# A decoder step on one core: prompt's compression moved ahead of the key stage, stick-breaking sums in rounded parts

## The reference

```python
def sb_attend(q, k, v, q_pos, k_pos):
    z = einsum('bqhd,bshd->bhqs', q, k) / sqrt(HEAD_DIM)
    mask = k_pos[None, :] < q_pos[:, None]
    log_1m = where(mask, log_sigmoid(-z), 0.0)
    after = cumsum(log_1m, axis=3, reverse=True) - log_1m
    a = where(mask, exp(log_sigmoid(z) + after), 0.0)
    return einsum('bhqs,bshd->bqhd', a, v)

def nsa_compress(kv, w_ck1, w_ck2, w_cv1, w_cv2, pe_k, pe_v):
    # 16-token chunks, blocks of two chunks: 31 blocks for the prompt, 127 for a sample
    ...
    kc = mlp(blocks[:, :, :, 0], pe_k, w_ck1, w_ck2)   # silu((x + pe) @ w1) @ w2
    vc = mlp(blocks[:, :, :, 1], pe_v, w_cv1, w_cv2)
```

## Time and profile before

| | |
|---|---|
| runs | 1195.89, 1203.27, 1191.61 us; median 1195.89 |
| profiled execution | 1194.02 us, of which the span of the profile 1192.2 us |
| mean granted clock of TensorE | 0.942 |
| PE, DVE, ACT busy | 91%, 51%, 32% of the span |

### The profile page before, as it was taken

The page is one execution under the profiler, slowest core; times in us unless marked ns, Lnnn a source line. Parts: engine busy times, 40 slices in busy tenths (PEclk is TensorE's granted clock), DMA queues, the critical chain, the costliest instruction groups (busy, mean ns, idle before and its releaser), DMA issues.

```text
span 1192.2 us, 22997 instructions
## 1 busy us (share of the span) xinstructions
PE 1084.8 (91%) x8348; PEld 951.0 (80%) x8348; DVE 605.8 (51%) x1026; ACT 382.4 (32%) x707; POOL 70.7 (6%) x83
## 2 busy tenths in 40 slices
PE   3996998988999999999999888999999999999993
PEld 2896998877888888555556557999999999999993
DVE  4331674776787782565345446445543335553332
ACT  4111112332333333545444445322231112321223
POOL 2000001111111110000000000110000000000002
PEclk9999997999899895899989998999999999999997
DMA  6529217999999942166766661323332333332221
GB/s 245 181 79 221 78 40 201 260 254 258 277 259 276 249 154 82 56 202 195 227 201 204 208 222 37 89 71 88 88 106 89 90 87 88 90 101 72 89 72 72
DMA packets 180131, 177.61 MB, mean 149 GB/s; under 512 B 13063, under 2 KB 140676, under 8 KB 177700
## 3 DMA queue, kind: packets, MB, share of 16 engines
q1 hardware_dynamic: 178610, 171.33, 50.3%
q10 hardware_dynamic: 1458, 5.43, 1.4%
HBM read 170.83 MB, written 10.06 MB: 152 GB/s over the span
## 4 chain that ended last, share of the span: by engine, by line
PE 64%; SPq 19%; issue 7%; DMA 4%; ACT 3%; DVE 3%; POOL 0%; POOLq 0%; ACTq 0%; DVEq 0%
PE bank L658 60%; SPq L572 4%; PE bank L662 4%; SPq L493 4%; SPq L532 3%; SPq L535 3%; SPq L486 2%; SPq L560 2%; DMA low_arena<-in_cache_nsa_slc_kv_dram 1%; DMA high_arena<-in_w_in_dram 1%; DMA high_arena<-in_x_sample_dram 1%; ACT low_arena L1528 1%; DMA high_arena<-in_cache_sb_kv_dram 0%; SPq L499 0%; SPq L501 0%
## 5 line engine op out<-in xcount | busy, mean ns | idle before, releaser
L658 PE MATMUL bank<-high_arena 128*128 128x254 f32 (+9 forms) x1864 | 238.7, 343 | 15.7 <-DMA high_arena<-in_cache_sb_kv_dram 6.9
L658 PEld LDWEIGHTS bank<-high_arena 128*128 128x128 f32 (+5 forms) x1864 | 185.7, 152 | 53.2 <-issue 13.5
L662 PE MATMUL bank<-low_arena 128*128 128x128 f32 (+3 forms) x658 | 104.8, 302 | 35.5 <-DMA low_arena<-in_cache_nsa_slc_kv_dram 18.0
L2083 DVE TENSOR_TENSOR w_low<-high_arena,w_high 128x1024 fp32r<-128x1024 f32 x72 | 90.1, 1251 | 85.4 <-ACT w_high L1465 73.8
L662 PEld LDWEIGHTS bank<-low_arena 128*128 128x128 f32 (+3 forms) x658 | 84.9, 160 | 46.8 <-issue 29.6
L1465 ACT ACTIVATE w_high<-high_arena 128x1024 fp32r<-128x1024 f32 x72 | 76.3, 1060 | 114.8 <-PE bank L658 113.7
L658 PE MATMUL bank<-a_high,w_high 128*128 128x256 f32 (+1 forms) x512 | 104.2, 285 | 5.3 <-issue 2.9
L658 PE MATMUL bank<-h_high,w_high 128*128 128x256 f32 (+1 forms) x512 | 103.6, 284 | 1.8 <-DVE h_low L2110 1.8
L658 PE MATMUL bank<-h_high,w_low 128*128 128x256 f32 (+1 forms) x512 | 103.8, 284 | 0.0
L658 PE MATMUL bank<-h_low,w_high 128*128 128x256 f32 (+1 forms) x512 | 103.8, 284 | 0.0
L658 PE MATMUL bank<-a_low,w_high 128*128 128x256 f32 (+1 forms) x512 | 103.7, 284 | 0.0
(11 more groups left out here) (207 smaller groups left out, 1533.8 us busy)
## 6 DMA issues: line engine op xcount, KB each, us to landing
low_arena<-in_cache_sb_kv_dram SPq DMA_DIRECT2D x128, 256.0 KB, 4.6
high_arena<-in_cache_sb_kv_dram SPq DMA_DIRECT2D x128, 256.0 KB, 3.4
high_arena<-in_cache_nsa_cmp_kv_dram SPq DMA_DIRECT2D x128, 128.0 KB, 5.0
high_arena<-in_w_up_dram SPq DMA_DIRECT2D x32, 512.0 KB, 4.0
high_arena<-in_w_down_dram SPq DMA_DIRECT2D x32, 512.0 KB, 4.2
high_arena<-in_w_in_dram SPq DMA_DIRECT2D x10, 1136.0 KB, 5.5
low_arena<-in_cache_nsa_slc_kv_dram SPq DMA_DIRECT2D x128, 64.0 KB
high_arena<-in_cache_nsa_slc_kv_dram SPq DMA_DIRECT2D x128, 64.0 KB, 2.3
```

Source lines behind the costliest of these rows:

```text
L658: return T.matmul(out, lhsT=l, rhs=r, start=start, stop=stop, **k)
L662: return T.transpose(out, in_, ident[0:n, 0:n])
L2083: V.tensor_tensor(w_lo_r[u], w_raw[u], w_hi[u], ALU.subtract).then_inc(sem(f"w_lo{u}"), 1)
```

## The change

1. The prompt's compression becomes the first unit of the key stage on PE, ACT, DVE and POOL. It is called `compress(0, 1, ...)`, and the semaphore counts of the samples' units are shifted by what it adds (`past`). Its chunks are loaded to the second buffer (`nat[1][0]`), by SP, after the stores of the prompt's compressed, selected and window keys and ahead of the store of its stick-breaking keys and values. POOL's permutations of a sample's first half now wait for PE's transposes of the unit before.
2. `sb_sum` no longer multiplies f32 soft sums with f32 masks. `sb_soft` writes to one buffer `sums`; ACT rounds it to fp32r (`sb_high`, into `z_parts`), DVE subtracts the rounded part from it and leaves the rest in fp32r too (`sb_low`, into `sums_low`), and PE multiplies both parts with rounded copies of the masks (`ntri_r`, `nones_r`): twice as many products, of one pass each. The rounded and the rest each have one buffer for a pair, in place of two buffers of sums. The masks are rounded by ACT once the sample scores have arrived. `rankA` moves to another place in memory.

```diff
-        spb = [z[:, NT, 0:2560].rearrange("p (h c) -> p h c", h=2), view(late_at, 2, 1280)]
+        sums = view(r_at, 2, 512)
+        sums_hi_r = rounded("z_parts", z_at, T5, COLS)[:, NT, 0:2560].rearrange("p (h c) -> p h c", h=2)
+        sums_hi = sums_hi_r.bitcast(F32)
+        sums_lo_r = rounded("sums_low", late_at, 2, 1280)
...
# SP
+            sp.wait_ge(sem("cmp_stored"), 16)
+            sp.dma_start(nat[1][0][0:2 * (NCP + 1)].rearrange("p t k h d -> p (t k h d)"),
+                O["cmp_p"][0, 0].rearrange("(c t) k h d -> c (t k h d)", t=CH // 2)).then_inc(sem("nat_in10"), 16)
             sp.dma_start(O["sb_p"][0, 0].rearrange("(t p) k h d -> p t (k h d)", p=P), z[:, 0:NT, O_KS:O_KS + 1024]).then_inc(sem("sb_stored"), 16)
...
-                        sp.wait_ge(sem("perm"), i * 8 + (4 * u + half) + 1)
+                        sp.wait_ge(sem("perm"), i * 8 + (4 * u + half + 2) + 1)
...
             load_keys(3, 0, True)
-            sp.wait_ge(sem("cmp_stored"), 16)
-            sp.wait_ge(sem("perm"), 4 * 6 + 3 + 1)
-            sp.dma_start(nat[0][0][0:2 * (NCP + 1)].rearrange("p t k h d -> p (t k h d)"),
-                O["cmp_p"][0, 0].rearrange("(c t) k h d -> c (t k h d)", t=CH // 2)).then_inc(sem("nat_in00"), 16)
             load_keys(3, 1, False)
...
# PE
+            compress(0, 1, lambda: None)
             with pe.Fori(0, 4) as i:
                 for u in range(2):
...
                     compress(i * 2 + u, 2, lambda: todo.pop(0)())
-            compress(B, 1, lambda: None)
...
             def sb_sum(m):
                 pr, i, n = sb_unit(m)
-                pe.wait_ge(sem("sb_sp"), m + 1)
-                for h in range(2):
-                    out = bank[2 * (m % 2) + h]
-                    ins = mm(out[:, 0:n], ntri, sp_tile(pr, i)[:, h], False, i == 3, skip_group_check=True)
-                    for j in range(3, i, -1):
-                        ins = mm(out[:, (j - i) * P:n], nones, sp_tile(pr, j)[:, h], False, j == i + 1, skip_group_check=True)
+                if m == 0:
+                    pe.wait_ge(sem("masks_in"), 2)
+                for part, ready in ((sums_hi_r, "sb_hi"), (sums_lo_r, "sb_lo")):
+                    pe.wait_ge(sem(ready), m + 1)
+                    for h in range(2):
+                        out = bank[2 * (m % 2) + h]
+                        for j in range(i, NT):
+                            ins = mm(out[:, (j - i) * P:n], nones_r if j > i else ntri_r, sp_tile(part, j)[:, h], False,
+                                     part is sums_lo_r and j == NT - 1, skip_group_check=True)
                 ins.then_inc(sem("sb_c"), 1)
...
# ACT
+            act.wait_ge(*signal("c_sc", 1))
+            for dst, name in ((ntri_r, "ntri"), (nones_r, "nones")):
+                ins = S.activation(dst, K(name), ACT.Copy)
+            ins.then_inc(sem("masks_in"), 1)
...
+            def sb_high(m):
+                pr, i, n = sb_unit(m)
+                act.wait_ge(sem("sb_sp"), m + 1)
+                if m:
+                    act.wait_ge(sem("sb_c"), m)
+                S.activation(sp_tile(sums_hi_r, i), sums[:, :, 0:n], ACT.Copy).then_inc(sem("sb_hi"), 1)
...
                     sb_exp(s - 1)
+                if s < SB_U:
+                    sb_high(s)
...
# DVE
                 dve.wait_ge(sem("sb_ln"), m + 1)
-                if pr >= 2:
-                    dve.wait_ge(sem("sb_c"), 4 * (pr - 1))
-                V.scalar_tensor_tensor(out=sp_tile(pr, i), in0=bank_pair(2 * (m % 2))[:, :, 0:n], scalar=0.0,
+                if m:
+                    dve.wait_ge(sem("sb_lo"), m)
+                V.scalar_tensor_tensor(out=sums[:, :, 0:n], in0=bank_pair(2 * (m % 2))[:, :, 0:n], scalar=0.0,
                                        in1=ebuf[:, m % 2, :, 0:n], op0=ALU.max, op1=ALU.add).then_inc(sem("sb_sp"), 1)
+            def sb_low(m):
+                pr, i, n = sb_unit(m)
+                dve.wait_ge(sem("sb_hi"), m + 1)
+                V.tensor_tensor(sp_tile(sums_lo_r, i), sums[:, :, 0:n], sp_tile(sums_hi, i), ALU.subtract).then_inc(sem("sb_lo"), 1)
...
                     acc_out(VALUE_ENDS.index(s - 1))
+                if 1 <= s < SB_U + 1:
+                    sb_low(s - 1)
                 small_steps(s)
...
# POOL
+            pool.wait_ge(sem("nat_in10"), 16)
+            for kv in range(2):
+                permute(1, kv, 0, 2 * (NCP + 1))
             for c in range(B):
...
+                        if half == 0:
+                            pool.wait_ge(sem("xT_mm0"), 4 * c + 2 * kv + 2)
+                        elif c:
+                            pool.wait_ge(sem("xT_mm1"), 4 * (c - 1) + 2 * kv + 2)
                         permute(c, kv, half, P)
-            pool.wait_ge(sem("nat_in00"), 4 * 128 + 16)
-            for kv in range(2):
-                permute(B, kv, 0, 2 * (NCP + 1))
```

More of the change, by code:

```diff
@@ L355, in decoder_step @@
         a1 = Fields(x_at, r_at)
-        r = Fields(r_at, small_at)
-        rankA = view(r.take(NSEL * NSEL), 3, NSEL // 3, NSEL)
+        r = Fields(r_at + 1024, small_at)
         ring = view(a1.take(8 * 512), 8, 512)
@@ L381, in decoder_step @@
         ident_r = rounded("ident_r", qsc_at, P)
+        ntri_r = rounded("ntri_r", kc_at, P)
+        nones_r = rounded("nones_r", kc_at + P, P)
         causal_r = rounded("causal_r", qsc_at + P, P)
@@ L445, in sb_unit, with sp_tile @@
             return m // 4, i, SEQ - i * P
-        def sp_tile(pr, i):
+        def sp_tile(part, i):
             lo = (0, 512, 896, 1152)[i]
-            return spb[pr % 2][:, :, lo:lo + SEQ - i * P]
+            return part[:, :, lo:lo + SEQ - i * P]
         def n_unit(n):
@@ L773, in compress @@
                 nb = n - 1 if tiles == 2 else NCP
+                past = int(tiles == 2)
                 def chunks_T(kv, s):
@@ L778, in chunks_T @@
                         return
-                    pe.wait_ge(sem("perm"), c * 4 + (tiles * kv + half + 1) + 1)
-                    pe.wait_ge(sem(f"xT_ev{s % 2}"), c * 4 + kv * 2 + s // 2 + 1)
+                    pe.wait_ge(sem("perm"), c * 4 + (tiles * kv + half + 1 + 2 * past) + 1)
+                    pe.wait_ge(sem(f"xT_ev{half}"), c * 4 + (kv * 2 + qp + 4 * past * (1 - half)) + 1)
                     for j in range(2):
@@ L790, in hidden @@
                     if qp == 0:
-                        pe.wait_ge(sem(f"hid_ready{kv}"), c + 1)
+                        pe.wait_ge(sem(f"hid_ready{kv}"), c + past + 1)
                     for half in range(tiles):
-                        pe.wait_ge(sem(f"xT_ev{half}"), c * 4 + kv * 2 + qp + 1 + 1)
+                        pe.wait_ge(sem(f"xT_ev{half}"), c * 4 + (kv * 2 + qp + 4 * past * (1 - half)) + 1 + 1)
                     out = bank[2 + kv][:, 0:KVH * nb].rearrange("p (h c) -> p h c", h=KVH)
@@ L818, in compress @@
                 between()
-                pe.wait_ge(sem("hid_ready0"), c + 1 + 1)
-                pe.wait_ge(sem("kvc_ev0"), c + 1)
+                pe.wait_ge(sem("hid_ready0"), c + past + 1 + 1)
+                pe.wait_ge(sem("kvc_ev0"), c + past + 1)
                 for hh in range(KVH):
@@ L1296, in chunks_out @@
                         return
-                    act.wait_ge(sem(f"xT_mm{half}"), c * 4 + kv * 2 + qp + 1)
+                    act.wait_ge(sem(f"xT_mm{half}"), c * 4 + (kv * 2 + qp + 4 * past * (1 - half)) + 1)
                     m = 64 if tiles == 2 else NCP + 1
@@ L1714, in silu @@
                 nb = n - 1
-                dve.wait_ge(sem(f"hid_e{kv}"), c + 1)
+                past = int(n == NCH)
+                dve.wait_ge(sem(f"hid_e{kv}"), c + past + 1)
                 e = hid[kv][:, :, 0:nb]
-                dve.wait_ge(sem(f"w2_mm{kv}"), c + 1)
+                dve.wait_ge(sem(f"w2_mm{kv}"), c + past + 1)
                 hp = bank[2 + kv][:, 0:KVH * nb].rearrange("p (h c) -> p h c", h=KVH)
@@ L1743, in _ @@
             dve.wait_ge(sem("cmp_stored"), 16)
+            silu(0, 0, NCP + 1)
+            silu(0, 1, NCP + 1)
+            compressed_out(0, kc[:, B, 0:NCP], vc[0:NCP, B, :], NCP + 1)
             with Turns(chain, 4, 2 * (NPG - 1)) as i:
@@ L2171, in permute @@
             def permute(c, kv, half, n):
-                if c:
-                    pool.wait_ge(sem(f"xT_mm{half}"), 4 * (c - 1) + 2 * kv + 2)
                 for hh in range(KVH):
@@ L2182, in _ @@
                         if kv == 0:
-                            pool.wait_ge(sem(f"nat_in{c % 2}{half}"), (c // 2 + 1) * 128)
+                            pool.wait_ge(sem(f"nat_in{c % 2}{half}"), (c // 2 + 1) * 128 + (16 if c % 2 and half == 0 else 0))
                         if c == 0 and half == 1:
                             pool.wait_ge(sem("sb_stored"), 16)
+                        if half == 0:
+                            pool.wait_ge(sem("xT_mm0"), 4 * c + 2 * kv + 2)
+                        elif c:
+                            pool.wait_ge(sem("xT_mm1"), 4 * (c - 1) + 2 * kv + 2)
                         permute(c, kv, half, P)
```

(3 more changed lines are left out.)

18 lines of the change are left out of this document (8 added, 10 removed).

## The result

The changed kernel takes 1188.1 us (median of 20 runs, 1180.2 to 1194.2), the kernel before 1195.1 in as many: a ratio of 0.9936, 95% interval 0.9916 to 0.9957. That is some 7 us; the forecast was 1178 and −15.7. Two later timings of the same kernel on other occasions gave 0.9888 [0.9827, 0.9950] and 0.9899 [0.9859, 0.9938]. That is 13 and 12 us. The gain is real; the three intervals together reach from 5 to 21 us, the first and longest timing alone from 5 to 10. Weighted by their intervals the three make some 9 us (an estimate). The forecast 15.7 lies outside the first interval and inside the two wider ones.

The account below looks back on a forecast made before the run. The prediction took PE to bound the stick-breaking stage and the stretch where the prompt's compression stands alone. From 1194.0 us, −8.8 (move) and −6.9 (sums) made −15.7, giving 1178; whole range 1168 to 1189.

Parts of the forecast that it names:

- The key stage: Prompt's unit moved from the key stage's end to its start: −19.3 us removed, +10.5 delay, net −8.8.
- rival 1: PE paces the key stage, so its 15.2 us delay passes whole: −4.1 us there, 1183 in all; chance 0.13.
- Price: Prompt's unit at the key stage's start costs PE 19.3 us, from 203.09 to 222.4.
- covered wait: PE's 4.13 us wait for the first sample's keys disappears behind the prompt's unit, making PE's delay 15.2 us.
- SP's wait: SP's queue in the key stage waits some 9 us for PE before its third quad.
- The products: Stick-breaking sums on PE: one-pass rounded products cost 24.0 us against 34.7 for two-pass f32, saving 10.7.
- Rival 2: Stick-breaking sums: weight loads are not covered, so one-pass products gain nothing, +1.4 us; 1187 in all; chance 0.10.
- given back 3.8: Stick-breaking stage: added copies, subtractions and longer page waits return 3.8 us of the sums' 10.7 saving.
- −6.9: Net forecast in us for the sums in the stick-breaking stage: −10.7 from products, 3.8 given back.
- no wait, but little room: Unit 5 (256 columns), stick-breaking: rest ready near 505.3, before PE's products; four such units at 0.2 us.
- the second half of rival 3: Low clock lasts 36 us from the last sample's end, covering 20 us more attention: +9, 1187; chance 0.07.
- Rival 4: Stick-breaking stage: hand-offs through three engines all show, +23.6 − 10.7 = +12.9 us, 1198 in all; chance 0.08.

Follow-up runs that it names:

- the kernel with the hand-offs and the old products: Changed kernel keeping copies, subtractions and their waits, but with two-pass f32 products on the rounded part, the rest left out; 0.9976 of the kernel before.
- no hand-off at all: Changed kernel with the soft sum written rounded and multiplied alone: no copy, no subtraction, the rest left out; 0.9848 of the kernel before.

## Why the prediction was wrong

**The key stage: right.** −8.8 was forecast. From the start of the last bias product to that of the scores the three profiles of the changed kernel have 256.0, 253.2 and 256.3 us. The eleven profiles in which the prompt's unit is moved and nothing else is added to this stage reach from 253.2 to 259.8, 256.7 in the mean, and the four in which it is not moved from 262.6 to 265.8, 264.6 in the mean: −7.9, and not the −4.1 of rival 1. Price, covered wait and SP's wait came as worked out. As a whole run the move brought 6.2 and 3.0 us in its two timings, each ±4 to 5.

**The products: right for PE.** 8 of the 10.7 us belong to steps 4 to 16; some 7 of PE's busy time were measured there, against the kernel with the hand-offs and the old products. Rival 2 falls.

**The step that failed: "given back 3.8".** In place of 3.8 us the sums gave back nearly all that PE saved: alone they measured 1.6 and 2.2 us under before, neither to be told from none, where −6.9 was forecast. By the kernel with hand-offs and the old products they cost some 4 us in steps 0 to 4 and 4.3 to 5.1 in steps 4 to 16, some 9 in all, by one profile. I priced unit 5's with "no wait, but little room": I took soft sum, copy and subtraction as if they followed each other, the rest ready 1.4 us behind the soft sum, and did not count what stands ahead of the subtraction in VectorE's order, 0.6 us of copy and 2.6 of ranking, although the order shown ahead of the prediction has that ranking right above it. The rest was ready 3.8 us behind the soft sum (494.33 to 498.16). PE idles 8.6 to 8.8 us of steps 4 to 16 in the three profiles of the changed kernel, 3.9 to 4.6 in the first of before and the two of the move, and the clock stands at 0.50 for 10.2 to 17.1 us there, where it did not fall in those three. Waits and clock together (4 to 5 us more of idling and, as an estimate, half of 10.2 us) make 9 to 10 us, no less than the 8 that the lighter products were to save there.

In steps 0 to 4 I had seen the copies on ScalarE's chain, at 1.1 us. The waits there hardly grew: PE's waits in these steps, first in before, then in the changed kernel:

```profile
PE bank L658 <- ACT high_arena L1383: 1.8, 2, 1.1
```

```profile
PE bank L662 <- ACT high_arena L1403: 1.8, 2, 1.2
PE bank L662 <- DVE sums_low L2012: 0.8, 2, 0.6
```

In the kernel with the old products they are 1.7 us and none is for the subtraction. So all but some 0.8 of the 3 to 4 us are the clock: the level stayed at 0.50 until 21 us behind step 0 (480.4), where it had risen after 12 in before (482.9). What fixes the moment of the rise stays open, and with it whether this part is a price of the hand-offs; my sum has no term for it.

The second part of that failure is that I took PE's saving for time as long as PE was busy most of it. In steps 4 to 16 PE idled 4.5 us of 81 before. I read this as PE binding; in truth several chains through ScalarE, VectorE and the pages ran just under PE. With early subtractions 11.2 us of idling are left, with no hand-off at all 9.3. So the 7 us that PE saved there bought 0 to 1 us against the move alone with the subtraction early (80.6 against 80.8 and 81.6), and 3 to 4 with it on GpSimd (77.8 and 78.1).

**Rivals.** The level in the attention stage did stay low longer, 21 us from step 0 in place of 12, as the second half of rival 3 has it, but not for the missing stretch ahead: products put in its place changed nothing, the sums alone show it with the stretch in place, and from its fall the low stretch got shorter (27.3 us for 37.5). Rival 4 was the right mechanism at under a third of its price for steps 4 to 16 (5.1 of 17.7): the subtraction is waited for at two units of twelve (3.9 us), the exponential at three (2.4 us, 0.3 in before). That 1188.1 lies inside the stated range, whose upper end is 1189, is luck: that end was set by rivals 1 to 3, and none of them happened as told there.

In sum, by the profiles: steps 0 to 16 took 102.5 and 106.7 us in before, 106.0 and 102.9 with the move alone, and 107.9, 105.0 and 104.2 with both: the sums brought nothing that these profiles can tell, where −6.9 was forecast, and the gain that can be told from none is the key stage's.

## What to carry to other kernels

When a value is to pass through one more engine before PE may use it, count every instruction that stands ahead of the new one in that engine's order, not only its own length. And before a saving on the busiest engine is booked as time, take the idle rows of the other engines and ask which chain is next: at 94% busy the next one can be a microsecond away. A quick test is the kernel with the new waits and the old work.

## What the runs showed of the hardware

A one-pass product of 128 columns does not need the 0.13 us that I took for its floor: the one that starts at 496.17 is followed by the next product at 496.23, 0.06 us later. I had taken the floor from durations (301 ns at 128 columns, 303 at 284), and records overlap. The 512-column product behind one of 128 takes more a column than the others: 0.28 us (486.77 to 487.05), 0.55 ns a column, against 0.36 us for the 768 columns of `nones_r` behind it (487.05 to 487.41), 0.47 ns; why is not shown.

Each of these products has its own load of 128 columns in the trace (0.19 us), and one head's part of four takes 0.64 us. The Trainium skill, "TensorE: Matmul & The Clock Gate", Part 3, The mechanism, in its list of what overlaps, lets a load overlap only products in another row group; the trace disagrees with its 0.64, for by that rule the four would take rival 2's 0.34 + 0.28 + 0.23 + 0.17 = 1.02.

The length of a wait alone did not tell whether the level of the clock would fall behind it. It fell behind waits of 2.2 and 2.3 us in the changed kernel's first profile, behind one of 1.5 in its third and behind one of 1.6 in both profiles of the sums alone; it did not behind the 1.7 of before and not behind the changed kernel's own two of 1.6. A fall lasted 3.4 to 10.2 us in these steps. At half speed that costs PE up to half of this time (an estimate), so that a fall can cost more than the wait ahead of it.
